# Gate tiles in the output stage, one-pass exponents, and the matrix memory's norms as wide operations

## What is computed

```
# mLSTM, per direction, chunk and head
s = (q @ k) * exp(log_d - m_row)             # log_d: masked decay matrix
h = num / max(|den|, exp(-m_row))
h = h * rsqrt(mean(h*h) + eps) * norm_g      # over the 128 values of a head
y_b = sum over the two directions of h, times sigmoid(o_pre)
# RWKV-7 output, per direction
gn = (out - mu) * rsqrt(var + GN_EPS) * ln_w + ln_b
y_a = (gn + bonus, summed over directions) * (sigmoid(gd) @ g_up)
# merge
merged = sigmoid(gate_a) * (y_a @ w_branch_a) + sigmoid(gate_b) * (y_b @ w_branch_b)
x = x + gt1 * (merged @ w_out)
```

## Time and profile before

| | us |
|---|---|
| median of 3 executions | 2765.51 (2765.45 to 2766.88) |
| the profiled execution, its own time | 2750.76 |
| span of its core, first to last instruction | 2749.0 |
| busy: PE / DVE / ACT / POOL | 2534.6 / 1318.8 / 1025.4 / 814.1 |
| granted TensorE clock, mean over the span | 0.958 of full |

### The profile page before, as it was taken

One profiled execution on the slowest core, in us unless ns is written; L12 is line 12 of the kernel. 1 busy time (PEld: TensorE's weight loads), 2 busy tenths in 40 slices (PEclk: granted clock), 3 DMA queues, 4 the chain that ended last, 5 costly groups with the idle time before them and its releaser, 6 DMA issues.

```text
span 2749.0 us, 53275 instructions
## 1 busy us (share of the span) xinstructions
PE 2534.6 (92%) x19772; PEld 2091.0 (76%) x19772; DVE 1318.8 (48%) x2667; ACT 1025.4 (37%) x1769; POOL 814.1 (30%) x659
## 2 busy tenths in 40 slices
PE   7998849599967996999899999999999999999997
PEld 3884439399946874888788888878888888888886
DVE  5764355665553322799644444420034444444443
ACT  4222444433333213322366666643232222222222
POOL 2420054543403432555555555524410000000000
PEclk8999769799988998999999999999999999999999
DMA  6541000000003222333344445554445555555551
GB/s 255 195 157 38 1 1 1 1 2 0 0 25 126 99 84 84 110 115 104 113 169 171 168 171 202 198 212 155 143 170 196 200 184 192 202 186 190 201 189 61
DMA packets 163766, 348.59 MB, mean 127 GB/s; under 512 B 13352, under 2 KB 79400, under 8 KB 161648
## 3 DMA queue, kind: packets, MB, share of 16 engines
q1 hardware_dynamic: 163696, 347.65, 35.8%
HBM read 276.30 MB, written 71.30 MB: 126 GB/s over the span
## 4 chain that ended last, share of the span: by engine, by line
PE 49%; DMA 1%; SPq 0%; ACT 0%; DVE 0%; issue 0%; ACTq 0%; DVEq 0%
PE ps_a L85 9%; PE ps_a L87 8%; PE ps_a L86 8%; PE ps_y L85 6%; PE ps_y L86 6%; PE ps_y L87 6%; PE ps_w L2373 4%; DMA w_scratch<-w_block 0%; DMA a_scratch<-act 0%; PE ps_y L2593 0%; DVE mixed L2554 0%; SPq L2457 0%; SPq L2462 0%; ACT L2526 0%; SPq L2452 0%
## 5 line engine op out<-in xcount | busy, mean ns | idle before, releaser
L85 PE MATMUL ps_a<-h_hi,u_hi 128*128 128x512 f32 x1024 | 407.5, 398 | 12.3 <-issue 5.6
L2544 DVE TENSOR_TENSOR v_lo<-v_raw,v_hi 128x1024 fp32r<-128x1024 f32 x128 | 158.2, 1236 | 535.8 <-ACT v_hi L2502 535.8
L86 PE MATMUL ps_a<-h_hi,u_lo 128*128 128x512 f32 x1024 | 401.4, 392 | 0.0
L87 PE MATMUL ps_a<-h_lo,u_hi 128*128 128x512 f32 x1024 | 401.3, 392 | 0.0
L2502 ACT ACTIVATE v_hi<-v_raw 128x1024 fp32r<-128x1024 f32 x128 | 135.8, 1061 | 478.4 <-PE ps_a L87 470.1
L85 PE MATMUL ps_y<-gated_hi,v_hi 128*128 128x512 f32 x768 | 299.4, 390 | 3.1 <-DVE gated_lo L2546 3.1
L86 PE MATMUL ps_y<-gated_hi,v_lo 128*128 128x512 f32 x768 | 299.5, 390 | 0.0
L87 PE MATMUL ps_y<-gated_lo,v_hi 128*128 128x512 f32 x768 | 299.4, 390 | 0.0
L85 PEld LDWEIGHTS ps_a<-h_hi,u_hi 128*128 128x128 f32 x1024 | 194.4, 190 | 51.1 <-issue 13.0
L1898 ACT ACTIVATE act<-ps_a 128x512 f32<-128x512 f32 x128 | 76.5, 598 | 398.0 <-PE ps_a L87 387.7
L87 PEld LDWEIGHTS ps_a<-h_lo,u_hi 128*128 128x128 f32 x1024 | 193.8, 189 | 41.0
(11 more groups left out here) (499 smaller groups left out, 5329.0 us busy)
## 6 DMA issues: line engine op xcount, KB each, us to landing
u_raw<-in_uT SPq DMA_DIRECT2D x128, 512.0 KB, 3.5
v_raw<-in_v SPq DMA_DIRECT2D x128, 512.0 KB, 4.9
a_scratch<-act SPq DMA_DIRECT2D x128, 256.0 KB, 2.2
w_scratch<-w_block SPq DMA_DIRECT2D x8, 4096.0 KB, 11.9
w_ring<-w_scratch SPq DMA_DIRECT2D x64, 512.0 KB, 4.4
gated<-a_scratch SPq DMA_DIRECT2D x128, 256.0 KB, 4.9
mg_raw<-in_w_merge SPq DMA_DIRECT2D x36, 512.0 KB, 3.4
vM<-in_ada_rows SPq DMA_DIRECT2D x32, 512.0 KB, 4.8
```

The costliest lines, as they stand in the source:

```text
L85: pe.matmul(out, wh, xh, start=first, stop=False)
L86: pe.matmul(out, wl, xh, start=False, stop=False)
L87: return pe.matmul(out, wh, xl, start=False, stop=last)
L2544: v.tensor_tensor(vl[:, q], v_raw[:, q], vh[:, q], ALU.subtract).then_inc(v_lo, 1)
```

## The change

It has three parts.

**One-pass exponents.** The four operands of the exponent matmuls get float32r copies, which PE multiplies in one pass. The gate row is split in a high part (rows 0 to 35) and a low part (rows 64 to 99) under a doubled selector; rows 32 to 63 get zeros. ACT makes four of the copies, POOL three copies of zeros (32x512, counted by `gaps`), DVE the high and low row.

**Norms as wide operations.** POOL divides `hc` by the denominator (eight multiplies of 128x512 with `dn`), ACT squares 512 columns at once (eight squares, spread between the copies of the next step), DVE reduces to four sums (`reduce`, eight), and the multiply by `dn` behind the root goes.

**Gate tiles in the output stage.** h, the weight buffers and the four `o_pre` tiles move from `phase_merge` to `phase_rwkv_output`. The low part of h goes from DVE to POOL. `evac` moves ahead of the eight multiplies on DVE. Merge begins with its fifth weight tile, waits for y only at its third tile, and the gating of y_b stands at its start; the x load (2 MB) stays in merge. `clear_semaphores` moves from behind the output stage to ahead of it. `fC`, `kk`, `qa`, `G` and the state lie at the other end of SBUF, so that their room can be used again; what is computed with them stays.

```diff
 def phase_rwkv_output(nc, a, b, h_dram, mg):
...
         def _(sp):
+            for k in range(2):
+                sp.dma_start(mg.h[:, 4 * k:4 * k + 4], h_dram[:, 4 * k:4 * k + 4]).then_inc(h_in[k], 16)
+                mg.load(sp, k, k)
             sp.dma_start(g_up[:], a["g_up"]).then_inc(vec_in, 16)
+            for n in range(2, O_TILES + 2):
+                sp.wait_ge(mg.w_lo, n - 1)
+                mg.load(sp, n % 2, n)
...
+        def _(g):
+            mg.rest(g, 0, 0)
+            for n, q in enumerate(quarters):
+                g.wait_ge(h_hi, n + 1)
+                g.tensor_tensor(b.h2l[:, q], mg.h[:, q], b.h2h[:, q], ALU.subtract).then_inc(h_lo, 1)
+            for n in range(1, O_TILES + 2):
+                mg.rest(g, n % 2, n)
...
+            for n in range(O_TILES):
+                act.wait_ge(mg.w_mm, n + 1)
+                mg.split(act, n % 2, n // 2 + 1)
+                act.activation(mg.sg[:, n], ps[n][:], ACT.Tanh, scale=0.5).then_inc(mg.o_tanh, 1)
...
             mm.then_inc(gate_mm, 1)
+            o_tile(0)
             pe.wait_ge(vec_in, 16)
...
             mm.then_inc(gate_mm, 1)
+            for n in range(1, O_TILES):
+                o_tile(n)
...
 def phase_mlstm(nc, a, b):
...
+            for u in range(0, UNITS, TX // P):
+                g.tensor_copy(sel_r[32:LOW, u:u + TX // P].rearrange("r u p -> r (u p)"), blank).then_inc(gaps, 1)
+            g.tensor_copy(neg_r[32:LOW], blank).then_inc(gaps, 1)
+            for n in range(2 * n_x):
+                i, z = n // 2, n % 2
+                g.wait_ge(den_done, n + 1)
+                d = dn[:, z, i if z == 0 else n_x - 1 - i]
+                g.tensor_tensor(outer(n), outer(n), d.unsqueeze(2).to_broadcast([P, MH, DV]), ALU.mult).then_inc(divided, 1)
...
-                pe.matmul(out[:].rearrange("p (n t) -> p n t", t=MC), b.ident[:], wide, start=True, stop=False)
-                pe.matmul(out[:], select[:, z * MH + h, :], b.neg_m[:], start=False, stop=True).then_inc(e_mm, 1)
+                wide = mask_r[:, z].unsqueeze(1).to_broadcast([P, n_x, MC])
+                pe.matmul(out[:].rearrange("p (n t) -> p n t", t=MC), ident_r[:], wide, start=True, stop=False)
+                pe.matmul(out[:], sel_r[:, z * MH + h, :], neg_r[:], start=False, stop=True).then_inc(e_mm, 1)
...
+            def squares(n):
+                act.wait_ge(divided, n + 1)
+                if n >= 2:
+                    act.wait_ge(reduced, n - 1)
+                act.activation(square[:, n % 2], outer(n), ACT.Square).then_inc(sq_done, 1)
...
                     inter(n)
-                if i:
-                    squares(i - 1)
-            squares(n_x - 1)
+                    if i and (n - first_x) % per in (per // 2 - 1, per - 1):
+                        squares(2 * (i - 1) + (n - first_x) % per // (per // 2))
+            for n in range(2 * n_x - 2, 2 * n_x):
+                squares(n)
...
+            v.wait_ge(gaps, 3)
+            v.tensor_copy(neg_r[0:GROWS], b.neg_m[:]).then_inc(parts_dve, 1)
+            v.wait_ge(parts_dve, 1)
+            v.tensor_tensor(neg_r[LOW:LOW + GROWS], b.neg_m[:], neg_r[0:GROWS], ALU.subtract).then_inc(parts_dve, 1)
...
                     state(n)
                     add(n)
+                if i:
+                    for n in range(2 * (i - 1), 2 * i):
+                        reduce(n)
                 v.wait_ge(sum_done, per * (i + 1))
...
 def phase_merge(nc, a, b, mg):
...
                         pe.wait_ge(w_lo, merge_tile(i, k, q) + 1)
+                        if q == 2:
+                            pe.wait_ge(y_lo, 2)
```

More of the change, by code:

```diff
@@ L1033, in _, with __init__, load, split @@
                     v.tensor_copy(b.state[:, g], st[g][:]).then_inc(state_in, 1)
-def phase_rwkv_output(nc, a, b):
+O_TILES, PART = MH, 3
+N_TILES = O_TILES + PART * KT + KT
+class MergeWeights:
+    def __init__(self, nc, ctx, a, b):
+        sb = alloc(nc, ctx, "right")
+        self.a = a
+        self.h = sb("mg_h", [P, KT, TX])
+        self.raw = sb("mg_raw", [P, 2, KT, P])
+        self.wh, self.wl = sb("mg_w_hi", [P, 2, KT, P], F32R), sb("mg_w_lo", [P, 2, KT, P], F32R)
+        self.sg = sb("mg_sg", [P, 4, TX])
+        self.raw_in = [b.semaphore(nc, f"mg_raw{k}") for k in range(2)]
+        self.w_hi, self.w_lo, self.w_mm, self.o_tanh = (b.semaphore(nc, f"mg_{n}") for n in ("w_hi_done", "w_lo_done",
+                                                                                             "w_mm", "o_tanh"))
+    def load(self, sp, k, tile):
+        sp.dma_start(self.raw[:, k], self.a["w_merge"][tile]).then_inc(self.raw_in[k], 16)
+    def split(self, act, slot, turns):
+        act.wait_ge(self.raw_in[slot], turns * 16 + 16)
+        act.activation(self.wh[:, slot], self.raw[:, slot], ACT.Copy).then_inc(self.w_hi, 1)
+    def rest(self, g, k, tile):
+        g.wait_ge(self.w_hi, tile + 1)
+        g.tensor_tensor(self.wl[:, k], self.raw[:, k], self.wh[:, k], ALU.subtract).then_inc(self.w_lo, 1)
+def phase_rwkv_output(nc, a, b, h_dram, mg):
     f = b.fX
@@ L1067, in _ @@
                 act.activation(sq[:, z, c], b.rwo[:, z, c], ACT.Square).then_inc(squared, 1)
+            for n, q in enumerate(quarters):
+                if n % 2 == 0:
+                    act.wait_ge(h_in[n // 2], 16)
+                act.activation(b.h2h[:, q], mg.h[:, q], ACT.Copy).then_inc(h_hi, 1)
+                if n % 2:
+                    mg.split(act, n // 2, 0)
             for n, (z, c) in enumerate(units):
@@ L1087, in _, with o_tile @@
                 pe.matmul(ps[n % 4][:], b.block_ones[:], sq[:, z, c], start=True, stop=True).then_inc(var_mm, 1)
+            def o_tile(n):
+                pe.wait_ge(mg.w_lo, n + 1)
+                pe.wait_ge(rooted, n + 5)
+                for j in range(KT):
+                    if n == 0 and j % 2 == 0:
+                        pe.wait_ge(h_lo, j // 2 + 1)
+                    mm = product(pe, ps[n][:], mg.wh[:, n % 2, j, :], mg.wl[:, n % 2, j, :], b.h2h[:, j, :], b.h2l[:, j, :],
+                                 j == 0, j == KT - 1)
+                mm.then_inc(mg.w_mm, 1)
             pe.wait_ge(bonus_in, 1)
@@ L1113, in _ @@
             v.tensor_scalar(gd[:], gd[:], 0.5, 0.5, ALU.mult, ALU.add).then_inc(gd_done, 1)
+            v.wait_ge(gate_mm, 1)
+            for c in range(PAIRS):
+                m = v.tensor_tensor(bonus[:, c], ps[4 + c][:], f[:, 8 + c, :], ALU.mult)
+            m.then_inc(evac, 1)
+            link(v.tensor_scalar(vecs[:, 2, :], vecs[:, 2, :], 2.0, None, ALU.mult))
             for n, (z, c) in enumerate(units):
@@ L1122, in _ @@
             link(m)
[L1123 to L1126, removed]
             v.wait_ge(evac, 1)
@@ L1502, in inter @@
                 m.then_inc(hi_done, 1)
[L1504 to L1512, removed]
+            def squares(n):
[3 more added lines that the diff above has]
+                act.activation(square[:, n % 2], outer(n), ACT.Square).then_inc(sq_done, 1)
+            act.activation(ident_r[:], b.ident[:], ACT.Copy).then_inc(parts_act, 1)
+            act.activation(mask_r[:], mask[:], ACT.Copy).then_inc(parts_act, 1)
+            act.activation(sel_r[LOW:LOW + GROWS], select[:], ACT.Copy).then_inc(parts_act, 1)
+            act.wait_ge(gaps, 2)
+            act.activation(sel_r[0:GROWS], select[:], ACT.Copy).then_inc(parts_act, 1)
             for h in range(MH):
@@ L1662, in phase_merge @@
         half = KT // 2
-        quarters = [slice(q * 2, q * 2 + 2) for q in range(KT // 2)]
+        ready = (O_TILES + 2) // 2
         def merge_tile(i, k, q):
```

127 lines of the change are left out of this document (60 added, 67 removed).

## The result

The changed kernel takes 2737.13 us (median of 10 runs, 2724.66 to 2750.21) against 2764.59 of before (10 runs); the ratio is 0.9906 with a 95% interval of 0.9877 to 0.9935, by the ratio 26 us less (18 to 34). 2731 was forecast. Its profiled execution has a span of 2728.1, 20.9 less than before's 2749.0.

The account below looks back on a forecast made before the run. PE was taken to bound the exponents, a PE-ACT ring the units, and waits of PE the output stage and merge. Terms 4.6 - 11.0 + 1.0 - 2.1 - 26.9 = -34.4 took 2765.51 to 2731 us; range 2718 to 2745.

Parts of the forecast that it names:

- C: Latent units of the mLSTM stage: DVE's waits and a half clock outweigh the removed squares; +1.0 us.
- A: Front of the mLSTM stage: DVE waits for POOL's three copies ahead of the context keys' weights; +4.6 us.
- D: Norms' tail after the last unit: wide reductions, divides and one square replace the sixteen last squares; -2.1 us.
- B: mLSTM exponents: one-pass matmuls cut a pair of products from 2.10 to 0.45 us; -11.0 us.
- E: Output stage and merge: gate tiles fill PE's waits for the gate product, h and y; -26.9 us.
- at the half clock, as it does now: mLSTM exponents: PE starts at half clock; staying there would make the exponents' gain -3.8 us.
- the rival where the clock never rises: mLSTM stage: one-pass products leave PE too little work for full clock; 2742 us, chance 0.15 shared with no one-pass gain.
- DVE waits out the divide: Latent units: POOL's 1.39 us divide blocks DVE, which runs late by 2.7 after steps two and three; 6.4 us in all.
- the rival of 0.27: Latent units: the clock holds, making the term -4.0 or -7.9 and the time 2726 or 2722 us; chance 0.27.
- I take it to fall in the first long wait: Latent units: the clock drops in PE's first 2.7 us wait; eight units at 2.52 cost 7.4 us more.
- POOL late with h: Output stage: POOL's five passes meet DVE's bonus instructions and end 12 us later; 2743 us, chance 0.12.
- from there on everything behind is the same program: Behind the merge's first tile that needs y's parts: nothing changes, so 0 us was forecast.

Follow-up runs that it names:

- e12: Kernel before plus one 128x512 product that nobody reads, in PE's 1.28 us wait at the mLSTM front; 2752.93 us, ratio 0.9956.
- e10: Changed kernel plus four 128x512 products that nobody reads, where PE stood 4.10 us at the mLSTM front; 2723.54 us, ratio 0.9862.
- e9: Changed kernel with the two reductions of a step's squares behind the step's denominators on DVE; single time 2725.37 us.
- e11: e8 plus one product that nobody reads in the 1.28 us wait of PE left at the mLSTM front; 2712.35 us, ratio 0.9816.
- e2: Changed kernel with the experts' weight buffers at the right end of SBUF beside h's parts; 2728.68 us, ratio 0.9877.
- e6: e2 with the query weights and the merge's y and merged parts also at the right end of SBUF; 2730.95 us, ratio 0.9859.
- e8: e6 with DVE's gate row split and its wait for POOL moved behind the context keys' weights and kept gates; 2723.79 us, ratio 0.9832.
- e13: Changed kernel with e3's late split, one filling product, pads before experts' buffers and y (remainder 0), query weights beside h (remainder 128); 2712.84 us, ratio 0.9823.
- e1: Kernel before with only h's high and low parts moved to the right end of SBUF; 2780.82 us, ratio 1.0068.
- e3: Changed kernel with DVE's gate row split and its wait for POOL moved behind the context keys' weights and kept gates; 2733.55 us, ratio 0.9908.
- e7: Kernel before with the experts' weight buffers at the right end of SBUF, h's parts left in place; single time 2798.61 us.
- e5: Kernel before with only the changed kernel's mLSTM stage (one-pass exponents, wide norms); 2745.16 us, ratio 0.9940.

## Why the prediction came out as it did

The time lies in the range and 6 us above the forecast, but by luck: in the profiled executions C came out 9.0 better than forecast, A and D 2.9 better and B 5.2 worse, and a cost of 17.8 was not in the sum at all. Measured in the two profiled executions, and in e12 and e10, where the clock is held at the front of both:

| term | forecast | after and before | e10 and e12 |
|---|---|---|---|
| A, front | +4.6 | +3.1 | +2.7 |
| B, exponents | -11.0 | -5.8 | -10.1 |
| C, units | +1.0 | -8.0 | -7.3 |
| D, norms' tail | -2.1 | -3.5 | -3.8 |
| E, output stage and merge | -26.9 | -26.9 | |
| behind the merge's first y product | 0 | +17.8 | |

(A runs from the stage's first product to the first exponent, B to the first inter product, C to the last add, D to y's scaling. The stage's later start, +0.9, and the scans, +1.5, complete the 20.9 by which the span is shorter; 34.4 was forecast.)

**A.** The mechanism was right and POOL's copy too dear: 0.58 instead of 1.1. **B.** The mechanism was right, the size and the clock not: a pair costs 0.66 at the full clock, not 0.45, since these matmuls start 0.33 apart (no run shows why not 0.227), and PE began "at the half clock, as it does now" but stayed there until 295, as in the rival where the clock never rises. With the clock held, the waits for DVE's keys are 0.63 and 0.55, and the sum is 10.1. **C** is the term that failed, in the size of its waits: 6.4 were forecast, two of 2.7 among them, and 3.0 came. The step in it that was wrong is "DVE waits out the divide" for whole instructions at every step. Only one tiny multiply does, in three steps of four, and the divide takes 1.04, not 1.39. (For a DVE that isn't blocked the working has two prices that don't agree: 4 less, and -7.9.) In the changed kernel's profile the clock held; that is the rival of 0.27, at its price for an unblocked DVE, -7.9. But that it held was a draw too. Behind a wait of 1.66 to 1.76 at a step's end the clock held in four cases (the changed kernel, e9, e10 and the first such wait of e11) and fell in five (e2, e6, e8, e11's second and e13). C then takes 30.6 (e11) and 33.2 (e13) instead of 29.2, and 38.0 to 38.4 in e2, e6 and e8, whose units also begin at half. So "I take it to fall in the first long wait" is neither shown nor refuted. PE of e10, then of e13 with the window behind its wait:

```profile
309.54 0.68 PE L1548 MATMUL ps_mu<-vM,ml_pw 128*128 128x129 f32 x4 [1.66 <-DVE mC L1665]
```

```profile
305.09 0.68 PE L1548 MATMUL ps_mu<-vM,ml_pw 128*128 128x129 f32 x4 [1.67 <-DVE mC L1664]
```

```profile
307.00:317.00 10.00, 10.00 (x50) 6.85 (x49) 5.75 (x16) 3.47 (x11) 2.08 (x2) 0.50 0.01 2
```

**D.** Right in its mechanism; the reductions, denominators and divides take 4.1 (328.28 to 332.42) instead of 5.4.

**E** was right to a tenth, and nearly so in each place. Shifted by the 11.82 by which the scans end earlier, the gate tiles end at 833.2 (833.3 forecast), h's parts at 806.5 (805.9), merge starts at 837.5 (837.1), and the first y product at 851.1 (851.1). One cause was wrong: the third tile did not stall for 3.3 behind x. ACT and POOL of the changed kernel, its weights' high and low part:

```profile
834.95 1.06 ACT L1060 ACTIVATE mg_w_hi<-mg_raw 128x1024 fp32r<-128x1024 f32 x1 [0.26 <-DMA mg_raw<-in_w_merge]
```

```profile
836.08 2.39 POOL L1064 TENSOR_TENSOR mg_w_lo<-mg_raw,mg_w_hi 128x1024 fp32r<-128x1024 f32 x1 [11.07 <-ACT mg_w_hi L1060]
```

The load came late, but the low part was done at 838.5, hidden by a first tile that took 2.75 longer at half. A stall that did not come and a half clock that was not forecast stand in for each other: the tenth is luck. The rival "POOL late with h" had the sign of the lock wrong: POOL kept its 2.50 and DVE's bonus took 8.2 more, which PE felt as 0.49.

That agrees with the Trainium skill ("SBUF — State Buffer", section "Who interferes with whom"), by which whoever issues first holds the shared ports for a whole instruction. The 1.05 beside the 1.04 is that rule in a row, though both start at 307.19 and the rows don't show which was issued first.

**What was missing** is the sentence "from there on everything behind is the same program". The program is the same, its addresses are not. In the changed kernel h and the experts' weights lie 384 bytes off a multiple of 512, and the 2400 products behind the route at 0.0056 more make 13.4; the stage lost 12.1. e1 has this cost without the rest of the change (684.2 for the stage). In e2, e6 and e13 the products are back at 0.2267 and the stage takes 674.1 to 674.4, against 671.5 before: 9.2 to 9.5 of the 12.1 go with the place, and no run shows where the rest comes from. The merge's y products add 1.3 (127.1 from the first of them to the first merged product; 125.7 to 125.8 in before, e6 and e13). The other 4.4 of the 17.8 lie around the route and at the end. Executions with the same places differ there by as much (e3 and e9 are 5 shorter than the changed kernel between the merge's first y product and the experts' stage), so their cause is open.

**The profiled executions** were two draws from a wide spread. In the ten traces without the filling product the clock fell at the front each time and rose again anywhere between 278 and not at all within the stage, old code or new. The one of before was among its luckiest (90.8 to the RWKV features, where e1 has 102.2 and e7 118.7). So B's -5.8 understates the change, and e5's 17 us (10 to 23) is the better figure for the mLSTM part; A to D of e10 and e12 add up to 18.5.

The best version, e11, with e13 beside it, beats both kernels: 2712.35, 1.8% under before and some 25 us under the change as made.

## What to carry to other kernels

When a change moves buffers, compare the starts of the matmuls behind it in both traces, and look at the remainder between their two operands, here by 512 bytes; the loss that a pad of 384 bytes mends is, at 19 us in e1 (13 to 25), about as large as the gain of both of the mLSTM's rewrites (17). Price a stage at both clock levels, since one profile shows one draw, and where a cheap product on data that nobody reads can fill PE's stand ahead of a long stage, try it first: it steadies every comparison after it.

## What the runs showed that was not expected

A matmul of 512 float32r columns starts every 0.2267 us when its moving and its stationary operand lie a multiple of 512 bytes apart, and every 0.229 to 0.2333 at remainders of 64 to 384 bytes. The Trainium skill ("SBUF — State Buffer", section "Who interferes with whom") gives PE a read port for either, independent of each other. No run shows what in the chip makes the difference, nor whether a multiple of 256 bytes would do as well; 128 does not (0.2325 in e13). The products of h with `w_in` ahead of the mLSTM stage lie at a remainder of 448 in every kernel here and take 0.233 at the mean; no run moved them.

And 1.28 us in which PE stands at the front cost the old stage up to 30 us (118.7 in e7 against 88.5 in e12): the clock then stayed at 0.50 although PE was busy all the time (26.00 of 26.00 from 274 to 300 in e1), while in e10, once at 1.00, it held through waits of 0.60 and 1.66, and in e13 it fell behind one of 1.67. What decides when it falls and when it rises again stays open.
